# Feed-forward weight groups multiplied in pairs, with Strassen's seven products in 11 blocks of the down projection

## What is computed

```python
def swiglu(h, w_gate, w_up, w_down):
    return (jax.nn.silu(h @ w_gate) * (h @ w_up)) @ w_down
...
x = x + swiglu(rmsnorm(x, norm_ffn_g), w_ffn_gate, w_ffn_up, w_ffn_down)
return rmsnorm(x, norm_final_g)
```

## Time and profile before

| | us |
|---|---|
| median of 3 runs | 1782.18 |
| lowest and highest | 1781.26, 1783.38 |
| the profiled execution, its own time | 1781.97 |
| its span, first to last instruction | 1779.5 |

### The profile page before, as it was taken

One profiled execution on the slowest core, in us unless ns is written; L12 is line 12 of the kernel. 1 busy time (PEld: TensorE's weight loads), 2 busy tenths in 40 slices (PEclk: granted clock), 3 DMA queues, 4 the chain that ended last, 5 costly groups with the idle time before them and its releaser, 6 DMA issues.

```text
span 1779.5 us, 20521 instructions
## 1 busy us (share of the span) xinstructions
PE 1765.7 (99%) x8052; PEld 1469.1 (83%) x8052; DVE 997.1 (56%) x1020; ACT 898.8 (51%) x1111; POOL 27.0 (2%) x51
## 2 busy tenths in 40 slices
PE   8999999999999999999999999999999999999998
PEld 7888888888888888888888888888888888888886
DVE  6577677655455554555665565555554445555554
ACT  6767668444545554544555464444443344444443
POOL 1000000000000000000000000000000000000000
PEclk9999999999999999999999999999999999999999
DMA  8565665666565756566755466666666666666654
GB/s 278 172 200 167 196 202 187 203 197 170 176 212 162 216 159 190 171 191 211 245 183 187 144 179 189 190 189 190 189 188 195 192 196 190 190 189 189 188 192 142
DMA packets 175740, 337.99 MB, mean 190 GB/s; under 512 B 10672, under 2 KB 15280, under 8 KB 175152
## 3 DMA queue, kind: packets, MB, share of 16 engines
q1 hardware_dynamic: 173232, 327.72, 60.9%
q0 software_dynamic: 1008, 5.24, 0.9%
q10 hardware_dynamic: 1424, 3.97, 0.6%
HBM read 334.80 MB, written 2.10 MB: 189 GB/s over the span
## 4 chain that ended last, share of the span: by engine, by line
PE 99%; DMA 0%; issue 0%; ACT 0%; DVE 0%; ACTq 0%; POOLq 0%; POOL 0%; DVEq 0%
PE group L383 31%; PE group L385 31%; PE group L384 31%; PE side L395 2%; PE side L496 0%; PE side L480 0%; DMA x_T_in<-in_x_T 0%; PE group L620 0%; PE group L618 0%; PE group L619 0%; PE side L451 0%; PE side L450 0%; PE side L449 0%; PE side L559 0%; PE side L478 0%
## 5 line engine op out<-in xcount | busy, mean ns | idle before, releaser
L972 DVE TENSOR_TENSOR w_lo<-w_raw,w_hi 128x1024 fp32r<-128x1024 f32 x612 | 747.6, 1224 | 713.1 <-ACT w_hi L646 711.8
L646 ACT ACTIVATE w_hi<-w_raw 128x1024 fp32r<-128x1024 f32 x612 | 647.0, 1060 | 809.2 <-PE group L385 785.0
L383 PE MATMUL group<-w_hi,x_hi 128*128 128x512 f32 x1628 | 638.2, 392 | 2.0 <-DVE w_lo L1020 2.0
L385 PE MATMUL group<-w_hi,x_lo 128*128 128x512 f32 x1628 | 634.4, 390 | 0.0
L384 PE MATMUL group<-w_lo,x_hi 128*128 128x512 f32 x1628 | 634.3, 390 | 0.0
L383 PEld LDWEIGHTS group<-w_hi,x_hi 128*128 128x128 f32 x1628 | 306.1, 188 | 64.5 <-issue 2.4
L385 PEld LDWEIGHTS group<-w_hi,x_lo 128*128 128x128 f32 x1628 | 306.1, 188 | 63.9
L384 PEld LDWEIGHTS group<-w_lo,x_hi 128*128 128x128 f32 x1628 | 306.1, 188 | 62.2
L383 PE MATMUL group<-w_hi,v_hi 128*128 128x512 f32 x320 | 125.2, 391 | 0.0
L385 PE MATMUL group<-w_hi,v_lo 128*128 128x512 f32 x320 | 124.6, 389 | 0.0
L384 PE MATMUL group<-w_lo,v_hi 128*128 128x512 f32 x320 | 124.5, 389 | 0.0
(11 more groups left out here) (245 smaller groups left out, 1058.5 us busy)
## 6 DMA issues: line engine op xcount, KB each, us to landing
w_raw<-in_w_in SPq DMA_DIRECT2D x223, 512.0 KB, 3.9
w_raw<-in_w_ffn_gate SPq DMA_DIRECT2D x88, 512.0 KB, 3.9
w_raw<-in_w_ffn_up SPq DMA_DIRECT2D x88, 512.0 KB, 3.7
w_raw<-in_w_ffn_down SPq DMA_DIRECT2D x88, 512.0 KB, 4.6
w_raw<-in_w_rnn_proj SPq DMA_DIRECT2D x32, 512.0 KB, 4.6
w_raw<-in_w_attn_proj SPq DMA_DIRECT2D x32, 512.0 KB, 4.3
w_raw<-in_w_mix_out SPq DMA_DIRECT2D x32, 512.0 KB, 4.2
w_raw<-in_w_xkv SPq DMA_DIRECT2D x16, 512.0 KB, 3.5
```

Source lines behind the costliest of these rows:

```text
L383: nc.tensor.matmul(gps[p][:, tt, :], xh[:, kt, tok], whi[:, s, k, :], start=kt == 0, stop=False)
L385: last = nc.tensor.matmul(gps[p][:, tt, :], xl[:, kt, tok], whi[:, s, k, :], start=False, stop=end)
L646: nc.scalar.activation(whi[:, s], raw[:, s], ACT.Copy).then_inc(hi_ready[s], 1)
L972: V_.tensor_tensor(wlo[:, s], raw[:, s], whi[:, s].bitcast(F32), ALU.subtract).then_inc(w_ready[s], 1)
```

## The change

**Pairs.** Gate group j and up group j are now one pair, and so are down groups 0 and 1, 2 and 3 of part a and 0 and 1 of part b. Down groups 2 and 3 of part b stay single, as in the kernel before. In a pair the chunks alternate: kp (two weight tiles by 512 columns) of the first group, the same kp of the second. Both PSUM buffers are filled side by side. A plan says what is done with each kp: `O` is an ordinary pair of chunks, `W` a block by Strassen's scheme.

**A W block** stands for the 2 x 2 block product (two token halves by two weight tiles, for both groups). It takes four slots, the steps A, B, C, D. A and B are loaded; C and D are filled by VectorE with three sums of weight tiles (`weight_sums`), in the raw slots. A, C and D are then split whole and B by half. TensorE runs 6, 3, 6 and 6 matmuls. Four of the seven products gather in the side buffers of PSUM over all W blocks of a pair (P1, Q5, P7, P6); they are combined after the last one by ScalarE (`first_fold`) and VectorE (`fold_rest`) into `fold` and added to x_res in two steps. The sums of the stationary operand are made once, when the inner columns are split (`sums_of`, `sums_lo`, `sums_hi`). 11 blocks are done so: 4 in each of two pairs, 3 in one.

**The end of a pair.** For gate/up, VectorE copies both groups out of PSUM into `fold` in the last step (`join`). ScalarE's tanh, in step 0 of the next pair, and VectorE's products (`inner_tok`, step 1) read from there. The transposes move from step 2 to step 3 of the next pair. For down, both groups are added in the last step.

All loops are unrolled. Semaphores between operations of VectorE itself are merged into one counter in the RNN and attention parts; the operations there stay the same.

```diff
+UP_PLAN = "O0 O1 O2 O3 O4 O5 O6 O7".split()
+DOWN_PLAN = {"a": "O0 O1 O3 W2 O5 W4 O7 W6 O9 W8 O10 O11".split(),
+             "b": "O0 O1 O3 W2 O5 W4 O7 W6 O8 O9".split()}
...
+        steps += [("O", kp, 0), ("O", kp, 1)] if step[0] == "O" else [("A", kp, 0), ("B", kp, 1), ("C", kp, None), ("D", kp, None)]
...
+            def pair(first, ws, row0, cols):
+                for c, (_, kp, half) in enumerate(STEPS[first]):
+                    if half is not None:
+                        load(N0[first] + c, ws[half], row0 + kp * CK * P, cols[half])
...
+                (p0, before0), (p1, before1) = buf_of(GI[first]), buf_of(GI[first] + 1)
+                for c, (kind, kp, half) in enumerate(steps):
+                    yield c, kind, kp
+                    if c < 2:
+                        pe.wait_ge(taken[(p0, p1)[c]], START + (before0, before1)[c])
+                    s, used = slot_of(N0[first] + c)
+                    pe.wait_ge(w_ready[s], START + used + 1)
...
+                    if kind == "A":
+                        products(P1, xh[:, k0, tok0], xl[:, k0, tok0], s, 0, begin, end)
+                        last = products(gps[p0][:, 0, :], xh[:, k1, tok0], xl[:, k1, tok0], s, 1, False, False)
+                    if kind == "B":
+                        last = products(gps[p1][:, 0, :], sh[:, w, 3, :], sl[:, w, 3, :], s, 1, False, False)
+                    if kind == "C":
+                        products(Q5, sh[:, w, 0, :], sl[:, w, 0, :], s, 0, begin, end)
+                        last = products(gps[p0][:, 1, :], xh[:, k1, tok1], xl[:, k1, tok1], s, 1, False, False)
+                    if kind == "D":
+                        products(P7, sh[:, w, 2, :], sl[:, w, 2, :], s, 0, begin, end)
+                        last = products(P6, sh[:, w, 1, :], sl[:, w, 1, :], s, 1, begin, end)
+                    last.then_inc(w_used[s], 1)
...
             def splits(n, count):
                 for c in range(count):
                     yield c
                     m = n + c + LEAD
...
+                        if KIND.get(m) == "A":
+                            weight_sums(m)
+                        ks = slice(1, 2) if KIND.get(m) == "B" else slice(0, CK)
...
+            def weight_sums(m):
+                for half in range(2):
+                    s, used = slot_of(m + half)
+                    dve.wait_ge(raw_full[s], 16 * (used + 1))
...
+                T1_T3 = tiles[:, 2 * c:2 * c + 3:2, :]
+                then(V_.tensor_tensor(T1_T3, tiles[:, a:a + 4:3, :], tiles[:, a + 2:a + 3, :].to_broadcast([P, 2, GW]), ALU.add))
+                then(V_.tensor_tensor(raw[:, d, 1], raw[:, c, 0], tiles[:, a + 3, :], ALU.add))
+                dve.sem_inc(raw_full[d], 16)
+                V_.tensor_tensor(raw[:, c, 1], raw[:, d, 1], tiles[:, a + 1, :], ALU.add).then_inc(raw_full[c], 16)
...
+            def join(first, half, end):
+                p, _ = buf_of(GI[first] + half)
+                wait_product(dve, end)
+                if last_sum(first) is None:
+                    V_.tensor_copy(fold[:, half], gps[p][:, :, :]).then_inc(taken[p], 1)
...
+                        if c == count - 1:
+                            join(first, 0, END[first])
+                            join(first, 1, END["up_" + part, j])
...
+                        if last_sum(first) is not None and c in (last_sum(first) + 3, last_sum(first) + 4):
+                            tt = c - last_sum(first) - 3
+                            cols = xres[:, tt, q * GW:(q + 2) * GW].rearrange("p (h n) -> p h n", h=2)
+                            then(V_.tensor_tensor(cols, cols, fold[:, :, tt, :], ALU.add))
+                        if c == count - 1:
+                            for h in range(2):
+                                add_group(GI["down_" + part, q + h], END["down_" + part, q + h], q + h)
```

More of the change, by code:

```diff
@@ L367, in _, with products, gemm_of @@
                 pe.sem_inc(signal, START)
-            def gemm(n, g, i, per_n, per_g, xh, xl, tiles, first=0):
-                p, before = buf_of(g, i, per_g)
+            def products(out, h, l, s, k, start, stop):
+                nc.tensor.matmul(out, h, whi[:, s, k, :], start=start, stop=False)
+                nc.tensor.matmul(out, h, wlo[:, s, k, :], start=False, stop=False)
+                return nc.tensor.matmul(out, l, whi[:, s, k, :], start=False, stop=stop)
+            def gemm_of(stage, j, xh, xl, tiles=KT, first=0):
+                p, before = buf_of(GI[stage, j])
                 for c in range(first, tiles // CK):
@@ L381, in gemm @@
                             tok = slice(tt * P, (tt + 1) * P)
[L382 to L385, removed]
+                            last = products(gps[p][:, tt, :], xh[:, kt, tok], xl[:, kt, tok], s, k, kt == 0, kt == tiles - 1)
@@ L566, in _, with inner_T @@
                         res_T("x2", GI["cross_out", j - 1], j - 1)
-            def inner_T():
+            def inner_T(i):
+                pe.wait_ge(sem("inner_tok"), i)
                 transpose(stage[0], side[0], "inner_T")
+            folds, sums_made, inners = 0, min(1, len(X_SUMS)), 0
+            pe.wait_ge(sem("x2_lo"), 2)
             for part, groups in (("a", FA), ("b", FB)):
[L572 to L602, removed]
-                        if q == 0 and c == 6:
-                            pe.wait_ge(sem("inner_lo"), done + groups)
@@ L636, in _, with splits @@
         def _(act):
-            def splits(n, count, i=0, per=0):
+            def splits(n, count):
                 for c in range(count):
@@ new lines, in _, with gate_tanh, inner_split @@
+            made = [0, 0, 0]
+            def gate_tanh(first):
+                wait_taken(act, GI[first])
+                for tt in range(TT):
+                    last = nc.scalar.activation(silu[:, tt, :], fold[:, 0, tt, :], ACT.Tanh, scale=hrstd["x2"][:, tt:tt + 1])
+                last.then_inc(sem("tanh"), 1)
+            def inner_split(kt0, summed):
+                made[0] += 1
+                act.wait_ge(sem("inner_T"), made[0])
+                if summed:
+                    nc.scalar.activation(f_in[:, :, :], side[0][:, 0:CK, :], ACT.Copy)
+                nc.scalar.activation(inner_hi[:, kt0:kt0 + NB, :], side[0][:, :, :], ACT.Copy).then_inc(sem("inner_hi"), 1)
@@ new lines, in sums_lo, with inner_tok @@
+            def sums_lo(dst, src, hi):
+                made[2] += 1
+                dve.wait_ge(sem("sums_hi"), made[2])
+                V_.tensor_tensor(dst, src, hi.bitcast(F32), ALU.subtract).then_inc(sem("sums_lo"), 1)
+            def inner_tok(first):
+                made[0] += 1
+                dve.wait_ge(sem("tanh"), made[0])
+                then(V_.scalar_tensor_tensor(silu[:, :, :], silu[:, :, :], 1.0, fold[:, 0], ALU.add, ALU.mult))
+                for tt in range(TT):
+                    last = V_.scalar_tensor_tensor(stage[0][:, tt, :], fold[:, 1, tt, :], silu_scale[:, tt:tt + 1], silu[:, tt, :], ALU.mult, ALU.mult)
+                last.then_inc(sem("inner_tok"), 1)
```

415 lines of the change are left out of this document (272 added, 143 removed).

## The result

The changed kernel takes **1826.38 us**, median of 4 runs (1824.34 to 1827.04), beside 1782.29 us for the kernel before on the same chip: a ratio of 1.0245, 95% interval 1.0228 to 1.0263, some 44 us slower. The profiled execution took 1826.01 us, with a span of 1823.9 us. The forecast was 1817, with a range of 1795 to 1835; the narrower range of its own mechanism alone, 1806 to 1826, ends 0.4 us short of the result.

The account below looks back on a forecast made before the run. TensorE bounds the kernel: number of matmuls times their pitch, plus its waits. Terms -7.5 + 13.2 + 11.4 + 17.9 = +35.0 on 1781.97 gave 1817 us, range 1795 to 1835 (own mechanism 1806 to 1826).

Parts of the forecast that it names:

- Matmuls removed: Down pairs: 11 W blocks issue 21 matmuls in place of 24, at 0.227 us each, -7.5 us.
- Ends of the gate/up pairs: Next pair waits for VectorE's PSUM copy, queued behind a low half: 1.2 us at each of 11 ends, +13.2 us.
- Ends of the down pairs: TensorE waits for late VectorE's folds and adds: 3.8 us at three ends, +11.4 us; 2.45 each if VectorE is on time.
- at the three down ends alone, +5: Smaller form of the clock rival: slower matmuls after the three down-end waits, +5 us, 1822 us; clock rival's chance 0.18.
- The larger form: Clock rival with falls at the down ends and the eight late O's, +18 us, 1835 us; clock rival's chance 0.18.
- Inside the W runs: Down pairs: TensorE waits for the chain of loads, sums and low halves around W blocks, +17.9 us together.
- Term (i): O pair behind a W waits for its load into A's and B's slots: 1.52 us late, 8 times, +12.2 us.
- Terms (ii) and (iii): Load-and-sum chain between W blocks: (ii) 0.9 us more, 5 times, +4.5; (iii) before a pair's second W, 3 times 0.4.
- Edits that cost nothing: Moved pair tail and transposes, unrolled loops, stationary-operand sums and merged semaphores: hidden, priced at no cost.
- loads are early enough: Rival: W runs keep TensorE's pace and VectorE is on time, +13 us, 1795 us; chance 0.12.
- The pair ends don't wait: Rival at step 0's wait for the first buffer: no pair-end waits, W runs at pace, 1774.5 us; chance 0.10.
- The clock falls: Rival: TensorE waits drop its clock to the 1.2 GHz level, 1.6 us more per fall, 1822 to 1835 us; chance 0.18.

Follow-up runs that it names:

- experiment 10: Changed kernel with both groups taken out of PSUM earlier, two spaced W per down pair, one W in ten gate/up pairs: 1770.19 us, ratio 0.9940.
- experiment 1: Changed kernel with the first group of each gate/up pair copied out of PSUM in the last step but one: 1811.4 us, ratio 1.0169.
- experiment 5: Changed kernel with each down-pair load fetching only 256 of its 512 columns (result not the layer's): 1794.84 us, ratio 1.0071.
- experiment 2: experiment 1 plus, in down pairs, first group added in the last step but one, second ahead of the fold addition in part a: 1795.93 us, ratio 1.0081.
- experiment 8: Changed kernel with 14 added matmuls of 512 columns at each of three down ends, into a free side buffer: 1819.16 us, ratio 1.0222.
- experiment 4: Changed kernel with ordinary chunks for all W blocks and groups taken out of PSUM as early as in experiment 2: 1780.48 us, ratio 0.9999.

## Why the prediction was right, and where a term was off

The side, the range and the three mechanisms that were priced (both kinds of pair end, the chain of loads) held; +35.0 was forecast and +44 came. Two things had no price in the sum: the clock, 5.7 us, and the restart behind a wait.

- **Matmuls removed**, -7.5: 33 less, and in experiment 10 the saving of 0.227 us each arrives in full.
- **Ends of the gate/up pairs**, +13.2: 13.4 by the trace, 13.5 by experiment 1. That they agree this closely is partly luck: the forecast counted from start to start, 1.2 us, where the starts show 1.04 (1134.87, for 1133.60 + 0.227), and the slower restart, which it left out, made up for it. The step was a second operation of VectorE in place, and it is in the timeline at 1132.45 as described.
- **Ends of the down pairs**, +11.4: 11.5 us of idle time in three, with the restart 12.5. The links of the 9.95 us can be read in VectorE's timeline, from the first fold (1382.19) to the release of TensorE, with the same additions and low halves between; experiment 5 gave the lower bound of 2.45 as well.
- **The clock**: the term that failed. The forecast's sum had nothing for it, though it had TensorE wait 3.8 us three times; the rival's form "at the three down ends alone, +5" is what happened, 5.7 us, the largest part of the 9 us that were missing. It was given 0.18 because a wait of 0.8 us had left the clock up. That row spoke for the short waits only, which is what experiment 2 and the windows below bear out; the row nearest to a wait of 3.8 us was the one of 1.95 us with its fall. The larger form, a fall at the late O's too, did not come: the windows of two periods of the W run, with their waits of 0.7 to 1.3 us, have a clock of 1.00:

```profile
1344.02:1356.87 12.85, 11.56 (x50) 8.89 (x49) 9.08 (x10) 5.94 (x6) 0.00 (x0) 1.00 0.49 163
1356.87:1369.96 13.09, 11.19 (x48) 8.32 (x46) 9.06 (x10) 5.83 (x6) 0.00 (x0) 1.00 0.49 161
```

  The Trainium skill (TensorE: Matmul & The Clock Gate, Part 1) has the half rate as the default, from which activity releases the engine; experiment 8 agrees, where added activity alone kept the clock at its upper level.
- **Inside the W runs**, +17.9: 19.4. The 14.6 us of idle time come in 14 entries for the 16 expected, each with a restart (0.34 us) that had no term; the idle time alone is 3.3 us less than forecast, so the two errors partly cancel. Term (i), 12.2 us in 8, measured 9.9 in 8, or 12.6 with the restart. Terms (ii) and (iii), 5.7 us in 8, measured 4.7 in 6, or 6.7: of the second W blocks only the one of part b waited, 0.49 us. The period shown is 12.84 us for 12.6: the landing took 4.0 us, not 3.8, and the sums 2.8, not 2.6 (1354.08 to 1356.87); the spacing of 1.6 us came out as forecast (4.8 us in three gaps).
- **The Trainium skill's figure for the load.** The first load of the four lands after 4.0 us, where the rows before had 3.8 and 3.5. The Trainium skill (DMA: Bandwidth & Descriptors, Anatomy of one DMA) has its fit, 2.0 us and the bytes over 436 GB/s, measured for loads issued through GpSimd, which the prediction didn't say; the loads here are issued by SP. It would give an estimate of 3.2 us for 512 KB, and of 2.6 us for the 256 KB loads of experiment 5. Those took 2.5 us, so the figure of the Trainium skill agrees with the half loads and is short for the whole ones. The measured figure decides; by that of the Trainium skill the forecast would have been 1803, farther from the result.
- **Edits that cost nothing**: experiment 4, within 0.1% of the kernel before, shows it for pairing, the moved transposes and the unrolled loops together.
- **Rivals**: "loads are early enough" is refuted for this kernel by the chain and by experiment 5, which had to halve the loads to get there. "The pair ends don't wait" is refuted by 14 entries; experiments 1 and 2 show what it takes. "The clock falls", in its smaller form, is what happened on top of the forecast, and the larger form is refuted.

Not tried: loads of the W blocks into more slots, so that a load need not wait for a low half.

## What to carry to other kernels

When two accumulations share both PSUM buffers, the copy out of PSUM loses the cover that alternating buffers gave: take the first one out as soon as it is complete, in the step before the last, and ahead of work that nobody waits for yet. A scheme that saves matmuls but fills buffers from other loads makes the chain from slot to load to sum to split longer than its share of busy time shows; put such blocks far enough apart that ordinary ones restore the lead. Price a wait of TensorE of some 4 us with the slower matmuls behind it too, and every wait with its restart.

## What the runs showed of the hardware

- A matmul stream that stopped for 3.5 to 4.2 us went on at the 1.2 GHz level for 3.4 to 5.2 us (0.43 us per matmul of 512 columns, not 0.227). In experiment 5, waits of 2.2 to 2.4 us at the same places left it up (the window behind the first end, in that kernel):

```profile
1382.90:1386.90 4.00, 3.99 (x17) 3.30 (x18) 2.23 (x2) 0.87 (x1) 0.00 (x0) 1.00 0.17 55
```

  Yet in that same execution a wait of 2.2 us near the start was followed by a fall (the window below), as one of 1.95 us was in the kernel before. So the length of the one wait doesn't decide alone; what else does was not tried.

```profile
13.50:16.50 3.00, 3.00 (x8) 2.32 (x8) 3.00 (x5) 3.00 (x6) 0.00 (x0) 0.50 1.03 361
```

- A wait of TensorE costs some 0.34 us beyond its idle time (1.22 for 0.88, over 11 ends). Experiment 4's kernel, with pairs but without these waits, needs 1780.5 us beside 1780.8 for the kernel before.
- In the changed kernel the 512 KB loads of w_ffn_down took 4.3 us from issue to landing at the median; the 256 KB loads of experiment 5 took 2.5 us.
